# A two-layer mLSTM and attention trunk: four neighbouring heads to an mLSTM step, decay rows through HBM

## The reference, cut to what matters

```python
b = jnp.cumsum(lfb, axis=-1)
inter = b + m[..., None]
dlog = b[..., :, None] - b[..., None, :] + igb[..., None, :]
dlog = jnp.where(causal, dlog, -jnp.inf)
m_t = jnp.maximum(inter, jnp.max(dlog, axis=-1))
w = jnp.einsum('bhtd,bhsd->bhts', qb, kb) * jnp.exp(dlog - m_t[..., None])
s_inter = jnp.exp(inter - m_t)
num = jnp.einsum('bhts,bhsv->bhtv', w, vb) + s_inter[..., None] * jnp.einsum('bhtd,bhdv->bhtv', qb, C)
den = jnp.sum(w, axis=-1) + s_inter * jnp.einsum('bhtd,bhd->bht', qb, n)
hout = num / jnp.maximum(jnp.abs(den), jnp.exp(-m_t))[..., None]
C_new = decay[..., None, None] * C + jnp.einsum('bhs,bhsd,bhsv->bhdv', ws, kb, vb)
```

## Time and profile before

| | us |
|---|---|
| median of 3 runs | 1155.17 (1154.96 to 1155.65) |
| the profiled execution's own time | 1156.1 |
| its span | 1154.3 |
| TensorE matmul busy | 1132.9 |
| VectorE busy | 543.5 |
| ScalarE busy | 431.9 |
| mLSTM steps, first decay rows to first output product | 115.94 to 202.09 |

### The profile page before, as it was taken

The page is one execution under the profiler, slowest core; times in us unless marked ns, Lnnn a source line. Parts: engine busy times, 40 slices in busy tenths (PEclk is TensorE's granted clock), DMA queues, the critical chain, the costliest instruction groups (busy, mean ns, idle before and its releaser), DMA issues.

```text
span 1154.3 us, 15362 instructions
## 1 busy us (share of the span) xinstructions
PE 1132.9 (98%) x5833; PEld 956.6 (83%) x5833; DVE 543.5 (47%) x834; ACT 431.9 (37%) x748; POOL 13.3 (1%) x22
## 2 busy tenths in 40 slices
PE   6999999999999999999999999999999999999997
PEld 6888888889888888888889988889888888888886
DVE  5434457864344344423356476646444434423344
ACT  6411225554323223323245266654332332423242
POOL 0000000000000000000000000000000000000000
PEclk9999999999999999999999999999999999999999
DMA  8232221422332333222262542002433233212241
GB/s 230 69 89 78 60 85 55 128 74 73 109 95 87 109 92 90 73 68 96 91 183 73 144 95 73 2 1 74 125 93 109 86 96 109 73 55 91 93 144 73
DMA packets 142984, 105.06 MB, mean 91 GB/s; under 512 B 22183, under 2 KB 130913, under 8 KB 142945
## 3 DMA queue, kind: packets, MB, share of 16 engines
q1 hardware_dynamic: 142944, 104.52, 30.8%
HBM read 102.41 MB, written 2.10 MB: 91 GB/s over the span
## 4 chain that ended last, share of the span: by engine, by line
PE 92%; DVE 4%; ACT 3%; DMA 1%; issue 1%; SPq 0%; DVEq 0%; ACTq 0%
PE ps L1312 18%; PE ps L1313 18%; PE ps L1314 18%; PE ps L1548 6%; PE ps L1549 6%; PE ps L1547 6%; PE ps L1651 2%; PE ps L1492 2%; PE ps L1494 2%; PE ps L1493 2%; PE ps L1377 1%; PE ps L1379 1%; PE ps L1378 1%; PE ps L1624 1%; PE ps L1635 1%; PE ps L1448 1%
## 5 line engine op out<-in xcount | busy, mean ns | idle before, releaser
L1312 PE MATMUL ps<-act_hi,w_hi 128*128 128x512 f32 (+1 forms) x1072 | 388.0, 362 | 1.4 <-DVE act_lo L848 1.4
L1313 PE MATMUL ps<-act_lo,w_hi 128*128 128x512 f32 (+1 forms) x1072 | 385.8, 360 | 0.0
L1314 PE MATMUL ps<-act_hi,w_lo 128*128 128x512 f32 (+1 forms) x1072 | 385.6, 360 | 0.0
L1312 PEld LDWEIGHTS ps<-act_hi,w_hi 128*128 128x128 f32 x1072 | 203.3, 190 | 33.4 <-DVE act_lo L848 2.2
L1314 PEld LDWEIGHTS ps<-act_hi,w_lo 128*128 128x128 f32 x1072 | 203.3, 190 | 30.1
L1313 PEld LDWEIGHTS ps<-act_lo,w_hi 128*128 128x128 f32 x1072 | 203.4, 190 | 29.7
L1547 PE MATMUL ps<-w_hi 128*128 128x512 f32 x288 | 112.0, 389 | 0.0
L1548 PE MATMUL ps<-w_lo,w_hi 128*128 128x512 f32 x288 | 112.0, 389 | 0.0
L1549 PE MATMUL ps<-w_hi,w_lo 128*128 128x512 f32 x288 | 112.0, 389 | 0.0
L671 ACT ACTIVATE arena<-ps,vecs 128x512 f32<-128x512 f32 x44 | 34.3, 780 | 188.9 <-PE ps L1314 188.9
L496 ACT CAST w_hi<-raw 128x1024 fp32r<-128x1024 f32 x71 | 73.4, 1047 | 84.3 <-PE ps L1314 45.0
(11 more groups left out here) (167 smaller groups left out, 1205.5 us busy)
## 6 DMA issues: line engine op xcount, KB each, us to landing
raw<-in_f_w_up SPq DMA_DIRECT2D x88, 512.0 KB, 4.5
raw<-in_f_w_down SPq DMA_DIRECT2D x44, 512.0 KB, 3.3
raw<-in_m_w_in SPq DMA_DIRECT2D x24, 512.0 KB, 3.8
raw<-in_m_w_out SPq DMA_DIRECT2D x8, 512.0 KB, 3.3
raw<-in_a_w_in SPq DMA_DIRECT2D x16, 256.0 KB, 4.4
raw<-in_a_w_out SPq DMA_DIRECT2D x16, 256.0 KB, 4.7
h<-in_x SPq DMA_DIRECT2D x4, 512.0 KB, 5.1
out<-h SPq DMA_DIRECT2D x3, 512.0 KB, 2.6
```

Of the source, the lines that this page charges most:

```text
L1312: nc.tensor.matmul(dst, lh, rh, start=(i == 0), stop=False)
L1313: nc.tensor.matmul(dst, lh, rl, start=False, stop=False)
L1314: last = nc.tensor.matmul(dst, ll, rh, start=False, stop=(i == n - 1))
```

## The change

A step now takes four neighbouring heads, 0 to 3 in the even steps and 4 to 7 in the odd ones (`four`), so its products change between even and odd heads from one to the next. Keys and inter products change between partitions 0 to 63 and 64 to 127 for their operands and between two banks for their outputs (banks 0 and 1, 3 and 4). State products change between output partitions 0 to 63 and 64 to 127. Intra products use banks 2 and 5, which also hold the state products.

The decay-row products go. GpSimd writes `u_rows` to HBM once and reads each chunk's 8 rows back to all partitions, 512 KB a chunk, into `g_post` and `g_pre` in turn (`u_all`). The loads of the mixer's gains into these two tensors move behind the fifth unit of output weights and wait until the last step's weights are made. VectorE's operations of `outputs` and `state` cover all four heads, or both halves of the partitions, in one instruction each. `squares` only takes the heads in the new order.

```diff
+        u_dram = nc.dram_tensor("u_dram", [NB, MH, P], F32, kind="Internal")
...
+        u_all = [g[:].rearrange("p (h t) -> p h t", h=MH) for g in (g_post, g_pre)]
...
-        decay_all = sb("decay_all", [P, MH, NB])
+        decay_own = sb("decay_own", [P, HG, NB])
...
-        def head(bank, place, t, pr=slice(None)):
-            bank, t = (bank, t) if t < HG - 1 else (5, place)
-            return ps[pr, bank, t * DV1:(t + 1) * DV1]
-
-        def heads(bank, place, pr=slice(None)):
-            three = ps[pr, bank, 0:(HG - 1) * DV1].rearrange("p (t v) -> p t v", v=DV1)
-            last = head(bank, place, HG - 1, pr).unsqueeze(1)
-            return [(slice(0, HG - 1), three), (slice(HG - 1, HG), last)]
+        def four(s):
+            return [(s % 2 * 2 + t, g, 4 * (s % 2) + 2 * t + g) for t in range(2) for g in range(2)]
+        INTRA, INTER = (2, 5), (3, 4)
+        STATE = slice(2 * DV1, 3 * DV1)
...
-            sp.wait_ge(zn_done, NB)
-            gains(norm_mix_post[0], norm_ffn_pre[0])
             for k in range(KT):
                 load_free(G_MOUT + k)
                 load(G_MOUT + k, m_w_out[0, k * P:(k + 1) * P])
+                if k == 4:
+                    sp.wait_ge(e_raw, NS)
+                    gains(norm_mix_post[0], norm_ffn_pre[0])
...
+            def u_everywhere(c):
+                nc.gpsimd.dma_start(u_all[c % 2], u_dram.ap()[c].partition_broadcast(P))\
+                    .then_inc(u_in[c % 2], 16)
+            pool.wait_ge(row_ready, 2)
+            nc.gpsimd.dma_start(u_dram.ap().rearrange("c h t -> h c t"),
+                                u_rows[:].rearrange("h (c t) -> h c t", t=P)).then_inc(u_out, 16)
+            pool.wait_ge(u_out, 16)
+            pool.wait_ge(zn_done, NB)
+            for c in range(2):
+                u_everywhere(c)
             for n in range(O_UNITS):
+                if n in (2, 4):
+                    pool.wait_ge(e_raw, n)
+                    u_everywhere(n // 2 + 1)
...
-            link(nc.vector.tensor_copy(decay_all[:].rearrange("p h c -> p (h c)"),
-                                       ps[:, 3, 0:MH * NB]))
+            for g in range(2):
+                pr = slice(g * DK, (g + 1) * DK)
+                nc.vector.tensor_copy(decay_own[pr], ps[pr, 3, 0:MH * NB]
+                                      .rearrange("p (t g c) -> p t g c", g=2, c=NB)[:, :, g])
...
             def weights(s):
-                c, g = s // 2, s % 2
-                dve.wait_ge(u_mm, s + 1)
-                for t in range(HG):
-                    hd = 2 * t + g
+                c = s // 2
+                dve.wait_ge(u_in[c % 2], 16 * (c // 2 + 1))
+                for t, g, hd in four(s):
                     ins = nc.vector.scalar_tensor_tensor(
-                        ew[:, s % 2, t], ps[:, 0, t * P:(t + 1) * P], gt[:, c, 0, hd:hd + 1], causal[:],
-                        ALU.add, ALU.min)
+                        ew[:, s % 2, 2 * g + t % 2], u_all[c % 2][:, hd], gt[:, c, 0, hd:hd + 1],
+                        causal[:], ALU.add, ALU.min)
                 ins.then_inc(e_raw, 1)
             def weigh(s):
                 dve.wait_ge(e_exp, s + 1)
                 dve.wait_ge(st_mm, s + 1)
-                nc.vector.scalar_tensor_tensor(
-                    ew[:, s % 2].rearrange("p t q -> p (t q)"), ps[:, 1], DK ** -0.5,
-                    ew[:, s % 2].rearrange("p t q -> p (t q)"), ALU.mult, ALU.mult).then_inc(w_done, 1)
+                e = ew[:, s % 2].rearrange("p (g t) q -> p g (t q)", g=2)
+                nc.vector.scalar_tensor_tensor(e, ps[:, 0:2, 0:2 * P], DK ** -0.5, e, ALU.mult,
+                                               ALU.mult).then_inc(w_done, 1)
             def state(s):
-                c, g = s // 2, s % 2
+                c, own = s // 2, slice(2 * (s % 2), 2 * (s % 2) + 2)
                 if c == NB - 1:
                     return
-                pr = slice(g * DK, (g + 1) * DK)
                 dve.wait_ge(n_mm, s + 1)
-                news = heads(4, 2, pr)
+                new = ps[:, INTRA[0]:INTRA[1] + 1:INTRA[1] - INTRA[0], STATE]
                 if c == 0:
-                    for ts, new in news:
-                        ins = nc.vector.tensor_copy(C[pr, ts], new)
+                    ins = nc.vector.tensor_copy(C[:, own], new)
                 else:
-                    dec = decay_all[pr, g::2, c].unsqueeze(2).to_broadcast([DK, HG, DV1])
-                    link(nc.vector.tensor_tensor(C[pr], C[pr], dec, ALU.mult))
-                    for ts, new in news:
-                        ins = nc.vector.tensor_tensor(C[pr, ts], C[pr, ts], new, ALU.add)
+                    dec = decay_own[:, own, c].unsqueeze(2).to_broadcast([P, 2, DV1])
+                    link(nc.vector.tensor_tensor(C[:, own], C[:, own], dec, ALU.mult))
+                    ins = nc.vector.tensor_tensor(C[:, own], C[:, own], new, ALU.add)
                 ins.then_inc(c_done, 1)
             def outputs(s):
-                c, g = s // 2, s % 2
+                c, hs = s // 2, slice(4 * (s % 2), 4 * (s % 2) + 4)
+                def products(banks):
+                    return ps[:, banks[0]:banks[1] + 1:banks[1] - banks[0], 0:2 * DV1]\
+                        .rearrange("p g (t v) -> p g t v", v=DV1)
                 dve.wait_ge(n_mm, s + 1)
-                out = v_tok[:, c].rearrange("p (t two) v -> p t two v", two=2)[:, :, g]
+                out = v_tok[:, c, hs].rearrange("p (t g) v -> p g t v", g=2)
+                scaled = itmp[:].rearrange("p (g t) v -> p g t v", g=2)
                 if c > 0:
-                    s_inter = gt[:, c, 2, g::2]
-                    for ts, inter in heads(3, 1):
-                        n = ts.stop - ts.start
-                        ins = nc.vector.tensor_tensor(
-                            itmp[:, ts], inter, s_inter[:, ts].unsqueeze(2).to_broadcast([P, n, DV1]),
-                            ALU.mult)
-                    link(ins)
-                for ts, intra in heads(2, 0):
-                    if c > 0:
-                        ins = nc.vector.tensor_tensor(out[:, ts], intra, itmp[:, ts], ALU.add)
-                    else:
-                        ins = nc.vector.tensor_copy(out[:, ts], intra)
+                    s_inter = gt[:, c, 2, hs].rearrange("p (t g) -> p g t", g=2)
+                    link(nc.vector.tensor_tensor(scaled, products(INTER),
+                                                 s_inter.unsqueeze(3).to_broadcast([P, 2, 2, DV1]),
+                                                 ALU.mult))
+                    ins = nc.vector.tensor_tensor(out, products(INTRA), scaled, ALU.add)
+                else:
+                    ins = nc.vector.tensor_copy(out, products(INTRA))
                 ins.then_inc(num_done, 1)
                 dve.wait_ge(num_done, s + 1)
-                den = out[:, :, DV]
+                den = v_tok[:, c, hs, DV]
                 link(nc.vector.scalar_tensor_tensor(dtmp[:], den, -1.0, den, ALU.mult, ALU.max))
-                link(nc.vector.tensor_tensor(dm[:, c, g::2], dtmp[:], gt[:, c, 3, g::2], ALU.max))
+                link(nc.vector.tensor_tensor(dm[:, c, hs], dtmp[:], gt[:, c, 3, hs], ALU.max))
...
-            def decays(s):
-
-                c, g = s // 2, s % 2
-                cs = slice(c * P, (c + 1) * P)
+            def keys(s):
+                cs = slice(s // 2 * P, (s // 2 + 1) * P)
                 if s >= 1:
                     pe.wait_ge(w_done, s)
-                for t in range(HG):
-                    hd = 2 * t + g
-                    ins = nc.tensor.matmul(ps[:, 0, t * P:(t + 1) * P],
-                                           ident[0:MH, hd:hd + 1].to_broadcast([MH, P]),
-                                           u_rows[:, cs], start=True, stop=True)
-                ins.then_inc(u_mm, 1)
-                pr = slice(g * DK, (g + 1) * DK)
-                for t in range(HG):
-                    ins = nc.tensor.matmul(ps[:, 1, t * P:(t + 1) * P], qk_t[pr, HG + t, cs],
+                for t, g, hd in four(s):
+                    pr = slice(g * DK, (g + 1) * DK)
+                    ins = nc.tensor.matmul(ps[:, g, (t % 2) * P:(t % 2 + 1) * P], qk_t[pr, HG + t, cs],
                                            qk_t[pr, t, cs], start=True, stop=True)
                 ins.then_inc(st_mm, 1)
             def combine(s):
-                c, g = s // 2, s % 2
+                c = s // 2
                 cs = slice(c * P, (c + 1) * P)
-                pr = slice(g * DK, (g + 1) * DK)
                 if s >= 1:
                     pe.wait_ge(num_done, s)
                     k = min(s, NS - 2)
                     pe.wait_ge(c_done, k)
                 if c > 0:
-                    for t in range(HG):
-                        nc.tensor.matmul(head(3, 1, t), qk_t[pr, t, cs], C[pr, t], start=True, stop=True)
+                    for t, g, hd in four(s):
+                        pr = slice(g * DK, (g + 1) * DK)
```

(27 more changed lines are left out.)

## The result

| | before | after | difference |
|---|---|---|---|
| median, us | 1155.41 (1154.96 to 1155.95, 4 runs) | 1141.47 (1141.35 to 1141.56, 4 runs) | -13.9 |
| profiled execution's own time | 1156.1 | 1141.44 | -14.7 |
| its span | 1154.3 | 1139.5 | -14.8 |
| end of intra(5) | 180.10 | 166.70 | -13.4 |
| first output product | 202.09 | 186.73 | -15.4 |

The ratio is 0.9879 (95% interval 0.9862 to 0.9896). Forecast were 1139.7 us and, against the profiled execution, 15.5 us less. The time lies at the upper end of the forecast's own range (1138.0 to 1141.5).

A forecast was written before the change was run, and what follows sets the result against it. TensorE was taken to bound the kernel; savings of 1.3 (step 0), 5.4, 2.2, 1.8, 2.6 (to intra(5)) and 2.2 us made 15.5, so 1140.6 profiled, 1139.7 median. Own range 1138.0 to 1141.5, whole range 1137.5 to 1146.0.

The forecast's parts named there:

- TensorE's groups: mLSTM steps up to intra(5): step 0 saves 1.3 us, decay groups 5.4, keys 2.2, inter 1.8, state 2.6.
- The scores of attention: Group in block 0 that already alternates row halves: 0.64 us from start to start, taken for keys and inter.
- Rival 1: State groups: column halves do not overlap, the group stays at 1.02 us; 1142.3 us in all, chance 0.27.
- alternation: Keys, inter and state groups: changing halves from product to product saves 0.44 us a group.
- VectorE: mLSTM steps: wider outputs and state operations take 0.75 us less a step; no stall in an ordinary step.
- The last two steps: From intra(5), t = 0: outputs(6) late, TensorE waits 1.4 us at intra(7), 2.2 of 3.9 us left.
- The gains: Output weights 5 to 7: gains in by t = 21.5, weight 5 due by 23.7, cover 1 us, cost nothing.
- The sign set for this: Output projection: waits for a DMA or cast of output weights over 1 us in sum would show the forecast wrong.
- Rival 2: Output projection bound by VectorE, ScalarE and output weights: last weight 4.65 us late, 1144.3 us, chance 0.12.
- The step down to the median: Whole kernel: profiled execution stood 0.9 us above the median of 1155.17, so 1140.6 became 1139.7 us.
- Rival 3: Keys and inter groups: alternation does not work here, only the decay rows go, 8.7 us; 1146.5 us, chance 0.06.
- rival 4: Weights in the mLSTM steps: broadcasts come late through GpSimd, slower than before, e.g. 1160 us; chance 0.03.

The follow-up runs named there:

- e4: Changed kernel with state, keys and inter products all in the first half, same count, shapes, banks and order: 1148.57 us.
- e3: Changed kernel with the decay rows made by TensorE again and no broadcasts through HBM, gains still late: 1146.68 us.
- e1: Changed kernel with the state products of a step in the order half 0, 0, 1, 1: 1141.97 us.
- e2: Changed kernel with keys and inter products in the order half 0, 0, 1, 1: 1141.52 us.
- e6: Changed kernel with the scaling of chunk 1's heads in step 6 done by ScalarE instead of VectorE: 1139.89 us.
- e8: Changed kernel with GpSimd's gate multiply of steps 5 and 6 cut to 2 of 512 columns: 1140.69 us.

## Why the prediction was right, and by how much it was off

**TensorE's groups.** Right in mechanism and size: up to intra(5) 13.3 us were forecast, 13.4 came. The scores of attention were the right row for both kinds of halves: keys and inter 0.64 to 0.65 (forecast 0.64), state 0.60 (0.58). e4 shows the 0.43 to 0.44 us a group, e3 the 6.5 us of the decay rows. Rival 1 fell with the 0.60. By the Trainium skill, TensorE: Matmul & The Clock Gate (Measured speedup vs the span model), column tiles gain about as much as row tiles; the trace agrees. By the same page of the Trainium skill (The mechanism) weight loads overlap matmuls in flight only across row groups, which would have kept the state group at 1.02 us; it took 0.60. What I had wrong is the word alternation: e1 and e2 show that the order is free.

**VectorE.** The forms came as interpolated: outputs 0.70 and 0.69, state 0.43 and 0.42 us. From the start of outputs to the start of weights it took 3.52 us in step 5 of the kernel before and takes 2.66 in step 4 after: 0.86 less, for 0.75 forecast.

**The last two steps.** Forecast: outputs(6) late, w_done(7) at t = 13.75, a wait of 1.4 us. It came at 180.33 + 0.69 - 166.70 = 14.32, a wait of 1.9. The cause forecast is shown by e6, where the wait falls to 0.31 once VectorE has 1.2 us less to do, and by e3 and e4, where TensorE is slower and does not wait at all. The 0.57 us on top is what the sum had at nothing: two places of VectorE stretch by 0.34 + 0.45 us beside GpSimd's multiply (e8), and 0.2 of that VectorE made up elsewhere.

From intra(5) to the first output product 2.2 us were to be left and 2.0 were. That the two agree so well is in part luck. The wait at intra(7) was half a microsecond longer than forecast, but the low half that was to come 0.3 us after TensorE was ready ended at 186.00 + 0.68 = 186.68, in time for the product at 186.73.

**The gains.** Costed at nothing with a cover of 1 us; this is the step that failed. The gains were to be in by t = 21.5 and weight 5 was to take 3.3 us and be there before t = 23.7. The second of the gains, issued at 183.36, was under way for 6.4 us, to t = 23.1; weight 5, issued at 186.10, took 5.02 and landed at t = 24.4. The last output weight landed 5.22 us after its release instead of 4.65. That is the whole of what the output projection gave back: 15.4 us of gain at the first output product and at that release were 14.8 at block 2's transposes. The sign set for this, over 1 us of waits for a DMA or a cast of the output weights, came by ScalarE's count (1.2 us in three waits; 0.7 in two before) and not by TensorE's (0.27). My error was to set only weight 5's deadline against the gains, at the 3.3 us of the median load. The last weight had the least cover in the kernel before, as the chain showed. That the gains are what held it up is likely but not shown: e3 has them late too, and there it took 4.2 us. Rival 2 had the place right and the price (4.65) far too high: 0.6 us came on top of the forecast.

**The step down to the median.** I took 0.9 us off since the profiled execution of before stood 0.9 above its median. The changed kernel's profiled execution stands at its median (1141.44 and 1141.47), so the medians differ by 0.9 us less than the profiled executions do. Together with 0.6 in the output projection, 0.1 ahead of it and 0.1 behind it, that makes the 1.8 us between 1139.7 and 1141.47. An offset of one execution is noise as much as the rest, and belongs in the range, not in the sum.

**Rivals 3 and 4.** Rival 3 fell with keys and inter at 0.64 us. For rival 4: the broadcasts through HBM land 3.9 and 5.1 us after issue (median of two each), VectorE never waits for them in weights, and the first two are issued at 58.37 and 58.92 us, over 55 us ahead of step 0.

```profile
g_post<-u_dram POOLq DMA_DIRECT2D x2, 512.0 KB, 3.9
g_pre<-u_dram POOLq DMA_DIRECT2D x2, 512.0 KB, 5.1
```

## What to carry to other kernels

If small fp32 products fill half the array's rows or columns, give a group of them work for both halves: here four products then took 0.60 to 0.65 us instead of 1.03 to 1.09, and how they were ordered within the group did not matter. The saving on the engine that bounds the kernel was exact (13.4 us for 13.3) until another engine had work there without slack. So look for the one stage in which that engine never waits, and count its time from a fixed event: here this gave the new wait to half a microsecond. When a load is moved, check every load behind it against its deadline, and price it as it runs with others in flight.

## What the runs showed of the hardware

- The two halves of the array ran at once with products in the order 0, 0, 1, 1: groups of 0.60 and 0.65 us as with 0, 1, 0, 1 (e1, e2), against 1.03 and 1.09 with one half (e4). So a product of half 1 starts before those of half 0 that stand ahead of it are done; this is inferred from the groups' length, since the trace does not name the half of a record.
- Column halves, which both read all 128 partitions of their moving operand, overlap in fp32 as fully as row halves do (0.60 us a group, 1.03 in e4).
- VectorE and GpSimd held each other up, depending on how their starts lay. A GpSimd multiply of 2 columns took 0.34 us at one place and 2.23 beside VectorE's head scalings (e8). The full one of 512 columns takes 0.77 in most steps and 1.68 to 2.02 beside the scalings (e3, after, before). In the changed kernel VectorE's 0.17 us operation took 0.51 and the pair of scalings 2.81 instead of 2.36; in before and e3, with other starts, VectorE kept its 0.17 and 2.36. No run varies the starts alone.
- A load of 512 KB was slower with two broadcasts of the same size ahead of it: weight 5 took 4.2 to 5.9 us in the eight traces with the gains ahead of it, and 3.1 to 3.6 in the four without.
